# Adding the gathered row pieces of the last stage on GpSimd and VectorE instead of on TensorE and VectorE

## The chip, the cores and the metric

The kernel runs on one core of one Trainium2 chip. The metric is device time in microseconds for one launch, the median of several runs. The engines of the core are written as in the profile: PE (TensorE), DVE (VectorE), ACT (ScalarE), POOL (GpSimd), SP (SyncE, which here only issues DMAs). SBUF is the on-chip memory that all of them read, PSUM the memory that PE writes its sums to.

## The reference

A two-layer transformer for 512 tokens of width 1024 (and 256 context tokens in the first layer), each layer ending in a mixture of 64 experts of which every token uses 8. All of it is float32. What is touched here is the very end of the second layer: the weighted outputs of a token's 8 experts are summed, scaled by a gate, added to the residual stream, and the result is normalised.

```python
def body(acc, blk):                      # over blocks of rows of one expert
    tok, w, e = blk
    xb = x_pad[tok]
    h = jax.nn.silu(xb @ w_gate[e]) * (xb @ w_up[e])
    return acc.at[tok].add((h @ w_down[e]) * w[:, None]), None
...
y = moe_ffn(f_lat, *moe_args)            # routed + shared
h_lat = h_lat + gt_fl * y.reshape(b, n, d)
...
return rmsnorm(h_lat, g_final)
```

## The kernel before

The program is a row of stages. Six of them (named A to I in the tiles' names) are attention and projections; a stage E ends each layer with the experts. It is `stage_moe(l, nt, ...)`, called with `nt = 6` tiles of 128 tokens in layer 0 and `nt = NL = 4` in layer 1. The second call is the last stage of the program, and there `final` is true. Only code under `final` is concerned.

The experts' stage works on groups `g = 0 ... NGR-1` of 128 rows (a row is one token for one expert). POOL gathers a group's rows by an indirect DMA, PE transposes them and multiplies them by the gate and up weights (L1618) and the down weights (L1632), ACT scales the result by the routing weight (L1786), and POOL scatters the 128 rows to `y_d` in DRAM by an indirect DMA (L1493), each to place token*8 + k. In the last stage the last three groups (`KEPT = 3`) are not scattered: their results stay in SBUF, as `kept[j]` (the tiles `E_yb` and `E_tmp`).

Then comes the tail, which sums for each tile `t = 0 ... 3` of 128 tokens the 8 rows of each token:

- SP loads 16 pieces of 1 MB, four a tile, each 128 tokens x 2 of the 8 rows x 1024 (L1464). Piece `n` of tile `t` lies in `y[t][n]` and bumps its own semaphore `s_p[4t+n]`. The pieces go where expert weights lay before (`E_gu`, `E_dn`, `fT`, `h`, `o`), so SP waits for the down product of that expert before it issues a piece. SP works in the order of the program and is the only issuer of these loads.
- DVE adds the pieces `n < PIECES - on_pe[t]` into `y[t][0]` (L1992, 128x2048 each), and then its two halves onto each other (L1993, 128x1024). With `on_pe = [1, 1, 2, 2]` it adds three pieces in tiles 0 and 1, that is two instructions, and two pieces in tiles 2 and 3, that is one.
- PE adds the last `on_pe[t]` pieces into PSUM by multiplying with the identity (L1742, 4 matmuls a piece in the code) and, in `add_kept`, the rows of the three kept groups by multiplying with a 0/1 matrix that picks a token's row (L1750, 6 matmuls a tile). The sum lies in `psA[t % 2]` (`E_psX` for tiles 0 and 2, `E_psG` for 1 and 3). From tile 2 on PE first waits for `s_acc >= 2(t-1)`, which DVE raises when it has read the buffer of two tiles ago.
- DVE normalises the tile before (`normed(t-1)`: reciprocal L1983 and a scaled product L1986, from `h` and `gain` in `E_tmp`), then, for each half `b` of 512 columns: add PE's sum from PSUM (L2002), multiply by the gate in `E_xT` (L2003), add into the residual `h` (L2004). ACT squares and sums `h` (L1850) and takes the root (L1851), which the next `normed` waits for. SP stores the tile (L1467).

`link` is a `Chain`: each linked DVE instruction raises a semaphore and DVE waits for it before it issues the next one. POOL has nothing to do in the tail: its last instruction is the last scatter, after which it waits for the scatters to land.

Of the kernel before, what the change touches and what calls it, by code (L numbers as in the profile page):

```python
# [11 lines left out]
ALU = mybir.AluOpType  # L12
# [7 lines left out]
NL, NT = SEQ // P, (SEQ + CTX) // P  # L20
# [12 lines left out]
NE, NG, TOPG, TOPK, FF = 64, 8, 4, 8, 256  # L33
# [123 lines left out]
def build(nc, a, out):  # L157
    with ExitStack() as whole:
# [8 lines left out]
        def sem(name):  # L167
            held.append(nc.alloc_semaphore(name))
            return held[-1]
# [16 lines left out]
        ident = cst[:, C_ID:C_ID + P]  # L186
# [33 lines left out]
        def bc(ap, n):  # L220

            return ap.unsqueeze(1).to_broadcast([ap.shape[0], n, ap.shape[1]])

        def bcl(ap, n):

            return ap.unsqueeze(len(ap.shape)).to_broadcast(list(ap.shape) + [n])
# [1038 lines left out]
        def stage_moe(l, nt, fT, lg, sel, su, o, raw):  # L1265
# [9 lines left out]
            NGR, runs = plan.groups, plan.runs  # L1275
# [3 lines left out]
            final = nt == NL  # L1279
            KEPT = 3 if final else 0  # L1280
            with ExitStack() as ctx:
                S = lambda n: sem(f"E{l}_{n}_s")
# [38 lines left out]
                v = flat[:, 0:nt * NE].rearrange("p (t e) -> p t e", e=NE)  # L1321
# [35 lines left out]
                if final:  # L1357
                    hot = T("hot", [P, NL, P])
                    hots = [[hot[:, t] for t in range(NL)], [x[:].rearrange("p t e -> p (t e)")[:, i * P:(i + 1) * P] for x in (lg, sel) for i in range(2)],
                            [x.rearrange("p t e -> p (t e)")[:, i * P:(i + 1) * P] for x, n in ((wt[:], 2), (tab[:], 1), (xi[:].bitcast(F32), 1)) for i in range(n)]]  # L1360
                    hotc = T("hotc", [P, KEPT, NL])
                    st = T("st", [P, NL, 3])
                    gate, gain = xT[:].rearrange("p k n -> p (k n)"), xb[:, (NGR - 3) % XB]
                    kept = [yb[:, (NGR - 3) % 2], yb[:, (NGR - 2) % 2], xb[:, (NGR - 2) % XB]]
                    psA = [psX[:].rearrange("p b k n -> p b (k n)"), psG[:]]
                    PIECES, on_pe = TOPK // 2, [1, 1, 2, 2]
                    homes = []
                    for p in range(NE - ring, NE):
                        gu, dn = slots[p % ring]
                        if p % ring == SHARED:  # L1370
                            gu, dn = None, None
                            whole = o[:].rearrange("p t d -> p (t d)")
                            homes += [(p, whole[:, 2 * D * n:2 * D * n + 2 * D]) for n in range(3)]
                        else:
                            two = gu.rearrange("p m k n -> p (m k n)")
                            homes += [(p, two[:, 0:2 * D]), (p, two[:, 2 * D:4 * D]), (p, dn.rearrange("p k n -> p (k n)"))]
                    homes = [(p, x.rearrange("p (k d) -> p k d", k=2)) for p, x in homes]
                    an = homes[PIECES * NL][1]
                    y = [[homes[PIECES * t + n][1] for n in range(PIECES)] for t in range(NL)]
                    choice_rows = y_d[1].rearrange("(t p k) d -> t p k d", p=P, k=TOPK)  # L1380
                    s_p = [S(f"p{n}") for n in range(PIECES * NL)]
                    s_hot, s_v, s_pe = S("hot"), S("v"), S("pe")
                    s_h, s_rt, s_an, s_acc, s_out, s_act = S("h"), S("rt"), S("an"), S("acc"), [S("out0"), S("out1")], S("act")

                s_wd_, s_gt, s_fold = S("wd_"), S("gt"), S("fold")
# [8 lines left out]
                s_xa, s_xv, s_sil, s_mul, s_hT, s_y = (S(n) for n in ("xa", "xv", "sil", "mul", "hT", "y"))  # L1394
# [10 lines left out]
                with nc.Block(no_gpsimd_drain=True) as block:  # L1405
# [72 lines left out]
                    def _(pool):  # L1478
                        G = nc.gpsimd
# [59 lines left out]
                                rows_out(g % 2, sca[:, g - 2:g - 1], s_sc[g % 2])  # L1539
                        for j in range(2):  # L1540
                            pool.wait_ge(s_sc[j], 16 * ((NGR - KEPT - j + 1) // 2))

                    @block.tensor
                    def _(pe):
# [189 lines left out]
                        for t in range(NL):  # L1734
                            if t >= 2:
                                pe.wait_ge(s_acc, 2 * (t - 1))
                            def add_pieces():
                                for n in range(PIECES - on_pe[t], PIECES):
                                    pe.wait_ge(s_p[PIECES * t + n], 16)
                                    for b in range(2):  # L1740
                                        for k in range(2):
                                            ins = nc.tensor.matmul(psA[t % 2][:, b], ident, y[t][n][:, k, b * 512:(b + 1) * 512],  # L1742
                                                                   start=(t == 0 and n == PIECES - on_pe[t] and k == 0), stop=(t > 0 and n == PIECES - 1 and k == 1))
                                return ins

                            def add_kept():
                                for b in range(2):
                                    for j in range(KEPT):
                                        pe.wait_ge(s_y, NGR - KEPT + j + 1)
                                        ins = nc.tensor.matmul(psA[t % 2][:, b], hots[j][t], kept[j][:, b * 512:(b + 1) * 512],  # L1750
                                                               start=(t > 0 and j == 0), stop=(t == 0 and j == KEPT - 1))
                                return ins

                            if t == 0:
                                add_pieces()
                                add_kept().then_inc(s_pe, 1)
                            else:
                                add_kept()
                                add_pieces().then_inc(s_pe, 1)

                    @block.scalar
                    def _(act):
# [91 lines left out]
                    def _(dve):  # L1854
                        link = Chain(dve, s_dve)
                        V = nc.vector
# [50 lines left out]
                        for t in range(nt):  # L1907
                            ins = V.max(v8[:, t], v[:, t])
                        link(ins)
                        for t in range(nt):  # L1910
                            ins = V.tensor_tensor(eq[:, t], v[:, t].unsqueeze(1).to_broadcast([P, 8, NE]), bcl(v8[:, t], NE), ALU.is_equal)
                        link(ins)
                        for t in range(nt):
                            ins = V.tensor_tensor(eq[:, t], eq[:, t], bc(wt[:, t], 8), ALU.mult)
# [47 lines left out]
                        for g in range(NGR):  # L1962
# [5 lines left out]
                            if final and g == 2:  # L1968
                                for j in range(KEPT):
                                    n = NGR - KEPT + j  # L1970
                                    for t in range(NL):
                                        ins = V.tensor_scalar(hotc[:, j, t:t + 1], gat[:, n:n + 1], -float(t * P), None, ALU.add)
                                link(ins)
                                for j in range(KEPT):
                                    for t in range(NL):
                                        ins = V.tensor_scalar(hots[j][t], cst[:, C_COL:C_COL + P], hotc[:, j, t:t + 1], None, ALU.is_equal)
# [4 lines left out]
                        def normed(t):  # L1981
                            dve.wait_ge(s_rt, t + 1)
                            link(V.reciprocal(st[:, t, 2:3], st[:, t, 1:2]))  # L1983
                            if t >= 2:
                                dve.wait_ge(s_out[t % 2], 16 * (t // 2))
                            V.scalar_tensor_tensor(an[:, t % 2], h[:, t], st[:, t, 2:3], gain, ALU.mult, ALU.mult).then_inc(s_an, 1)  # L1986

                        for t in range(NL):
                            for n in range(PIECES - on_pe[t]):
                                dve.wait_ge(s_p[PIECES * t + n], 16)  # L1990
                                if n >= 1:
                                    link(V.tensor_tensor(y[t][0], y[t][0], y[t][n], ALU.add))  # L1992
                            link(V.tensor_tensor(y[t][0][:, 0], y[t][0][:, 0], y[t][0][:, 1], ALU.add))  # L1993
                            if t == 0:
                                dve.wait_ge(s_v, 32)
                            if t >= 1:
                                normed(t - 1)
                            for b in range(2):
                                c = slice(b * 512, (b + 1) * 512)
                                ac = y[t][0][:, 0, c]  # L2000
                                dve.wait_ge(s_pe, t + 1)
                                link(V.tensor_tensor(ac, ac, psA[t % 2][:, b], ALU.add))  # L2002
                                link(V.tensor_tensor(ac, ac, gate[:, c], ALU.mult))  # L2003
                                V.tensor_tensor(h[:, t, c], h[:, t, c], ac, ALU.add).then_inc(s_acc, 1)  # L2004
                            dve.wait_ge(s_acc, 2 * t + 2)
                            dve.sem_inc(s_h, 1)
# [593 lines left out]
```

## Time and profile before

| | |
|---|---|
| median of 3 runs | 2600.85 us (2596.98, 2600.85, 2615.37) |
| profiled execution: its time, its span | 2595.15 us, 2593.4 us |
| PE busy | 2347.7 us, 91% |
| DVE busy | 836.2 us, 32% |
| ACT busy | 664.7 us, 26% |
| POOL busy | 272.9 us, 11% |
| HBM traffic over the span | 261 GB/s |
| mean granted PE clock | 0.968 |

The shares are averages over the whole program. The tail that is changed lies between about 2530 us and the end, some 60 of 2593 us, so the argument is made in that stretch alone. The profile ends 1.75 us before the profiled execution's own time, and that execution lies 5.7 us under the median.

### The profile page before, as it was taken

How to read it: one execution, taken by the hardware profiler on the slowest of the kernel's cores; microseconds unless marked ns; L12 is line 12 of the kernel's file. 1: busy time of each engine (PE TensorE's matmuls, PEld its weight loads, DVE VectorE, ACT ScalarE, POOL GpSimd, SP SyncE). 2: the span in 40 equal slices, each digit the busy share in tenths (PEclk: the TensorE clock that was granted, in tenths of full speed). 3: DMA queues.
4: the chain of work that ended last, by engine and by line, in shares of the span. 5: the costliest groups of instructions: out<-in, count | busy, mean ns of one | idle time of the engine just before them, and what ended most of it. 6: DMA issues, size and time to landing. Idle time of an engine off the chain costs nothing. (4 is left out here: it accounts for less than half of the span.)

```text
span 2593.4 us, 34211 instructions
## 1 busy us (share of the span) xinstructions
PE 2347.7 (91%) x13502; PEld 1242.5 (48%) x13502; DVE 836.2 (32%) x1740; ACT 664.7 (26%) x1443; POOL 272.9 (11%) x257
## 2 busy tenths in 40 slices
PE   7999999799899999999994779998889998889888
PEld 3544555475544333333331778887645333333333
DVE  2332556626510001000013955556363100000006
ACT  1111444521011211212112344445311121111111
POOL 1000000032011111111111000000111111111100
PEclk9999999999999999999997899999989999999999
DMA  8565900112479999999995711100337999999996
GB/s 334 196 228 202 345 23 1 70 65 111 186 288 357 378 382 397 390 371 384 381 336 210 274 45 38 37 31 1 143 126 312 413 419 419 419 419 410 413 373 281
DMA packets 130093, 661.90 MB, mean 255 GB/s; under 512 B 18691, under 2 KB 29955, under 8 KB 68240
## 3 DMA queue, kind: packets, MB, share of 16 engines
q1 hardware_dynamic: 101120, 574.04, 56.7%
q0 software_dynamic: 28816, 85.69, 8.4%
q8 instruction: 108, 1.77, 0.3%
q14 instruction: 49, 0.40, 0.0%
HBM read 604.38 MB, written 72.96 MB: 261 GB/s over the span
## 5 line engine op out<-in xcount | busy, mean ns | idle before, releaser
L1618 PE MATMUL E_psG<-E_gu,E_xT 128*32 128x512 f32 (+2 forms) x2544 | 530.4, 611 | 45.3 <-DMA E_gu<-in_we_up_dram 29.8
L1952 DVE TENSOR_TENSOR E_hh<-E_sil,E_psG 128x256 f32<-128x256 f32 x96 | 40.5, 422 | 1078.5 <-ACT E_sil L1780 1078.5
L1618 PEld LDWEIGHTS E_psG<-E_gu,E_xT 128*32 128x32 f32 (+2 forms) x2544 | 158.1, 122 | 286.5 <-issue 279.7
L1632 PE MATMUL E_psY<-E_dn,E_hT 128*32 128x512 f32 (+2 forms) x1272 | 261.9, 596 | 1.5 <-ACT E_hT L1783 1.5
L1618 PE MATMUL E_psG<-fT,E_xT 128*32 128x512 f32 (+2 forms) x704 | 237.4, 619 | 3.7 <-DMA E_gu<-in_we_up_dram 3.2
L1618 PE MATMUL E_psG<-o,E_xT 128*32 128x512 f32 (+2 forms) x736 | 225.8, 612 | 5.7 <-DMA E_gu<-in_we_up_dram 5.7
L1780 ACT ACTIVATE E_sil<-E_psG 128x256 f32<-128x256 f32 x96 | 36.8, 383 | 657.7 <-PE E_psG L1618 657.7
L1493 POOL DMA_INDIRECT y_d<-E_yb,E_sca x91 | 91.5, 1006 | 951.2 <-ACT E_yb L1786 951.2
L1786 ACT ACTIVATE E_yb<-E_psY,E_wgt 128x1024 f32<-128x1024 f32 x95 | 105.8, 1114 | 285.7 <-PE E_psY L1632 285.7
L1618 PE MATMUL E_psG<-raw,E_xT 128*32 128x512 f32 (+2 forms) x464 | 148.4, 594 | 1.2 <-DVE E_xT L1949 1.2
L150 PE MATMUL I_psC<-I_w_hi,I_aT_hi 128*128 128x384 f32 (+1 forms) x336 | 111.4, 332 | 20.0 <-DVE I_aT_lo L2293 16.5
L1611 PEld LDWEIGHTS E_psX<-cst,E_tmp 128*128 128x128 f32 x768 | 94.2, 193 | 73.2 <-issue 72.8
L660 PE MATMUL B_psC<-w_in,B_aT 128*128 128x288 f32 (+3 forms) x384 | 122.0, 473 | 2.0 <-ACT B_aT L404 2.0
L1632 PEld LDWEIGHTS E_psY<-E_dn,E_hT 128*32 128x32 f32 (+2 forms) x1272 | 71.9, 118 | 105.3 <-issue 97.8
L1632 PE MATMUL E_psY<-o,E_hT 128*32 128x512 f32 (+2 forms) x368 | 112.6, 596 | 0.0
L1611 PE MATMUL E_psX<-cst,E_tmp 128*128 128x128 f32 x768 | 109.2, 285 | 0.0
L151 PE MATMUL I_psC<-I_w_lo,I_aT_hi 128*128 128x384 f32 (+1 forms) x336 | 107.6, 320 | 0.0
L152 PE MATMUL I_psC<-I_w_hi,I_aT_lo 128*128 128x384 f32 (+1 forms) x336 | 107.6, 320 | 0.0
L1488 POOL DMA_INDIRECT E_tmp<-f_d,E_gat x94 | 94.9, 1010 | 37.9 <-issue 36.9
L932 ACT ACTIVATE C_prob<-C_psS,C_nmax 128x768 f32<-128x768 f32 (+3 forms) x96 | 67.7, 705 | 118.5 <-DVE C_nmax L874 60.6
L1192 POOL TENSOR_TENSOR h<-h,D_y 128x1024 f32<-128x1024 f32 x8 | 18.9, 2357 | 732.1 <-DVE D_y L1169 732.1
L1618 PEld LDWEIGHTS E_psG<-fT,E_xT 128*32 128x32 f32 (+2 forms) x704 | 65.3, 126 | 62.3 <-issue 60.4
(452 smaller groups left out, 3789.0 us busy)
## 6 DMA issues: line engine op xcount, KB each, us to landing
E_gu<-in_we_gate_dram SPq DMA_DIRECT2D x70, 1024.0 KB, 14.3
E_gu<-in_we_up_dram SPq DMA_DIRECT2D x70, 1024.0 KB, 21.3
E_dn<-in_we_down_dram SPq DMA_DIRECT2D x70, 1024.0 KB, 16.0
h<-in_w_ada_dram SPq DMA_DIRECT2D x40, 1024.0 KB, 4.8
o<-in_we_gate_dram SPq DMA_DIRECT2D x24, 1024.0 KB, 11.9
o<-in_we_up_dram SPq DMA_DIRECT2D x24, 1024.0 KB, 15.7
o<-in_we_down_dram SPq DMA_DIRECT2D x24, 1024.0 KB, 24.0
I_ring<-y_d SPq DMA_DIRECT2D x24, 1024.0 KB, 7.1
```

The costliest lines, as they stand in the source:

```text
L150: nc.tensor.matmul(acc, xh, wh, start=(start and i == 0), stop=False)
L151: nc.tensor.matmul(acc, xh, wl, start=False, stop=False)
L152: ins = nc.tensor.matmul(acc, xl, wh, start=False, stop=(stop and i == n - 1))
L660: ins = nc.tensor.matmul(acc[:, 0:n], aT[:, k], w_in[:, k, c0:c0 + n], start=(k == 0), stop=(k == KD - 1))
L932: nc.scalar.activation(prob[:, i % 3, 0:len(ks) * P], psS[:, i % 2, c0:512 + CTX], ACT.Exp, bias=nmax[:, Q, u:u + 1], accum_out=ssum[:, Q, ...
L1488: pool.indirect_dma_start(xb[:, j], None, f_d[l][0:nt * P], bass.IndirectOffsetOnAxis(ap=index.bitcast(U32), axis=0), bounds_check=nt * P ...
L1493: pool.indirect_dma_start(y_d[l], bass.IndirectOffsetOnAxis(ap=index.bitcast(U32), axis=0), yb[:, j], None, bounds_check=nt * P * TOPK - 1 ...
L1611: ins = nc.tensor.transpose(psX[:, k // 4, k % 4], x[:, k], ident)
L1618: ins = nc.tensor.matmul(psG[c:c + n, 0].rearrange("p (v f) -> p v f", v=2), xT[:, k, c:c + n], slots[s][0][:, :, k], start=(k == 0), stop ...
L1632: ins = nc.tensor.matmul(psY[c:c + w, n], hT[:, j, k, c:c + w], slots[s][1][:, k, n * 512:(n + 1) * 512], start=(k == 0), stop=(k == KF - 1))
L1786: nc.scalar.activation(rows.rearrange("p (b n) -> p b n", b=2), psY[:], ACT.Copy, scale=wgt[:, i]).then_inc(done, 1)
L1952: V.tensor_tensor(hh[:], sil[:], psG[:, 0, FF:2 * FF], ALU.mult).then_inc(done, 1)
```

## The change

`on_pe` is gone. In each of the four tiles

- POOL adds piece 1 into piece 0 (`y[t][0] += y[t][1]`), after waiting for the two pieces' landings, and raises the new semaphore `s_pair`,
- DVE waits for pieces 2 and 3, adds 3 into 2, waits for `s_pair`, adds piece 2 into piece 0, and adds the halves as before,
- PE adds the kept rows alone.

```diff
-                    PIECES, on_pe = TOPK // 2, [1, 1, 2, 2]
+                    PIECES = TOPK // 2
...
                         for j in range(2):
                             pool.wait_ge(s_sc[j], 16 * ((NGR - KEPT - j + 1) // 2))
+                        if final:
+                            for t in range(NL):
+                                for n in range(2):
+                                    pool.wait_ge(s_p[PIECES * t + n], 16)
+                                G.tensor_tensor(y[t][0], y[t][0], y[t][1], ALU.add).then_inc(s_pair, 1)
...
-                            def add_pieces():
-                                for n in range(PIECES - on_pe[t], PIECES):
-                                    pe.wait_ge(s_p[PIECES * t + n], 16)
-                                    for b in range(2):
-                                        for k in range(2):
-                                            ins = nc.tensor.matmul(psA[t % 2][:, b], ident, y[t][n][:, k, b * 512:(b + 1) * 512],
...
-                            if t == 0:
-                                add_pieces()
-                                add_kept().then_inc(s_pe, 1)
-                            else:
-                                add_kept()
-                                add_pieces().then_inc(s_pe, 1)
+                            for b in range(2):
+                                for j in range(KEPT):
+                                    pe.wait_ge(s_y, NGR - KEPT + j + 1)
+                                    ins = nc.tensor.matmul(psA[t % 2][:, b], hots[j][t], kept[j][:, b * 512:(b + 1) * 512], start=(j == 0), stop=(j == KEPT - 1))
+                            ins.then_inc(s_pe, 1)
...
                         for t in range(NL):
-                            for n in range(PIECES - on_pe[t]):
+                            for n in range(2, PIECES):
                                 dve.wait_ge(s_p[PIECES * t + n], 16)
-                                if n >= 1:
-                                    link(V.tensor_tensor(y[t][0], y[t][0], y[t][n], ALU.add))
+                            link(V.tensor_tensor(y[t][2], y[t][2], y[t][3], ALU.add))
+                            dve.wait_ge(s_pair, t + 1)
+                            link(V.tensor_tensor(y[t][0], y[t][0], y[t][2], ALU.add))
                             link(V.tensor_tensor(y[t][0][:, 0], y[t][0][:, 0], y[t][0][:, 1], ALU.add))
```

Place 1 is DVE at tile 2. Before (`E_dn`, `E_gu`, `E_gu`, `E_dn` are the tile's four pieces in order):

```order
L1992 TENSOR_TENSOR E_dn<-E_dn,E_gu 128x2048
L1993 TENSOR_TENSOR E_dn<-E_dn 128x1024
L1983 RECIPROCAL E_st<-E_st 128x1
L1986 SCALAR_TENSOR_TENSOR o<-h,E_st,E_tmp 128x1024
L2002 TENSOR_TENSOR E_dn<-E_dn,E_psX 128x512
```

and with the change:

```order
L1978 TENSOR_TENSOR E_gu<-E_gu,E_dn 128x2048
L1980 TENSOR_TENSOR E_dn<-E_dn,E_gu 128x2048
L1981 TENSOR_TENSOR E_dn<-E_dn 128x1024
L1970 RECIPROCAL E_st<-E_st 128x1
L1973 SCALAR_TENSOR_TENSOR o<-h,E_st,E_tmp 128x1024
```

DVE has one 128x2048 addition more here, and so in tile 3; in tiles 0 and 1 the count is the same, two, but the first of them now adds pieces 2 and 3.

Place 2 is PE at tiles 2 (`E_psX`) and 3 (`E_psG`), behind the kept rows. Before:

```order
L1750 MATMUL E_psX<-E_tmp,E_tab 128x512
L1742 MATMUL E_psX<-E_gu,cst 128x512 x4
L1742 MATMUL E_psX<-E_dn,cst 128x512 x4
L1750 MATMUL E_psG<-E_yb,E_hot 128x512
```

and with the change, the whole of tile 3 and the end of tile 2:

```order
L1745 MATMUL E_psX<-E_tmp,E_tab 128x512
L1745 MATMUL E_psG<-E_yb,E_hot 128x512
L1745 MATMUL E_psG<-E_yb,sel 128x512
L1745 MATMUL E_psG<-E_tmp,E_xi 128x512
L1745 MATMUL E_psG<-E_yb,E_hot 128x512
L1745 MATMUL E_psG<-E_yb,sel 128x512
L1745 MATMUL E_psG<-E_tmp,E_xi 128x512
```

The 24 matmuls by the identity (`cst`), 4 for each of 6 pieces, are gone. Place 3 is POOL behind its last two scatters, where nothing stood before:

```order
L1493 DMA y_d<-E_yb,E_sca 4096x1024 x2
L1546 TENSOR_TENSOR E_gu<-E_gu 128x2048
L1546 TENSOR_TENSOR fT<-fT,h 128x2048
L1546 TENSOR_TENSOR E_dn<-E_dn,E_gu 128x2048
L1546 TENSOR_TENSOR E_gu<-E_gu 128x2048
```

Four additions are new there, one a tile, both inputs in SBUF. The order of SP's DMAs is the same in both kernels.

## Rows read from the trace of the kernel before

**Rows 1.** The chain of waits, 2530 to 2594 us: start us, us, what

```profile
2540.50 3.63 PE E_psX L1742 x8
...
2575.03 6.88 PE E_psG L1742 x16
...
2587.92 1.28 DVE o L1986
```

**Rows 2.** The timeline of DVE, 2532 to 2594 us: start us, us, instruction

```profile
2537.47 2.29 DVE L1992 TENSOR_TENSOR E_gu<-E_gu,E_dn 128x2048 f32<-128x2048 f32 x1 [0.42 <-DMA E_dn<-y_d]
...
2549.42 0.69 DVE L2002 TENSOR_TENSOR E_gu<-E_gu,E_psX 128x512 f32<-128x512 f32 x1 [8.40 <-PE E_psX L1750]
...
2553.83 2.29 DVE L1992 TENSOR_TENSOR fT<-fT,h 128x2048 f32<-128x2048 f32 x1 [0.23 <-DVE h L2004]
...
2558.49 1.23 DVE L1993 TENSOR_TENSOR fT<-fT 128x1024 f32<-128x1024 f32 x1
...
2561.15 0.68 DVE L2002 TENSOR_TENSOR fT<-fT,E_psG 128x512 f32<-128x512 f32 x1
...
2565.55 2.29 DVE L1992 TENSOR_TENSOR E_dn<-E_dn,E_gu 128x2048 f32<-128x2048 f32 x1 [0.22 <-DVE h L2004]
...
2581.93 0.69 DVE L2002 TENSOR_TENSOR E_gu<-E_gu,E_psG 128x512 f32<-128x512 f32 x1 [1.93 <-PE E_psG L1742]
...
2585.43 0.69 DVE L2004 TENSOR_TENSOR h<-h,E_gu 128x512 f32<-128x512 f32 x1
```

**Rows 3.** The timeline of SP's DMA issues, 2500 to 2594 us

```profile
2533.28 0.43 SPq L1464 DMA_DIRECT2D h<-y_d  x1
2535.40 0.92 SPq L1464 DMA_DIRECT2D E_gu<-y_d  x2
...
2536.95 0.96 SPq L1464 DMA_DIRECT2D E_gu<-y_d  x2
...
2540.54 1.83 SPq L1464 DMA_DIRECT2D E_gu<-y_d  x2
...
2544.57 1.34 SPq L1464 DMA_DIRECT2D o<-y_d  x1
```

**Rows 4.** DMA issues in windows inside rows 3: KB each, us to landing

```profile
h<-y_d SPq DMA_DIRECT2D x1, 1024.0 KB, 14.3
...
E_gu<-y_d SPq DMA_DIRECT2D x1, 1024.0 KB, 16.8
...
E_gu<-y_d SPq DMA_DIRECT2D x1, 1024.0 KB, 20.6
...
E_gu<-y_d SPq DMA_DIRECT2D x1, 1024.0 KB, 26.6
...
o<-y_d SPq DMA_DIRECT2D x1, 1024.0 KB, 27.9
```

**Rows 5.** POOL's groups by form: xcount | busy us, mean ns | idle before

```profile
L1192 POOL TENSOR_TENSOR h<-h,D_y 128x1024 f32<-128x1024 f32 x8 | 18.9, 2357 | 732.1 <-DVE D_y L1169 732.1
L1505 POOL TENSOR_TENSOR o<-o,E_yb 128x2048 f32<-128x2048 f32 x2 | 9.0, 4498 | 6.7 <-DMA E_yb<-mod_d 6.6
```

**Rows 6.** The timelines of DVE and of POOL where both worked, layer 1

```profile
1883.07 2.49 DVE L1126 TENSOR_TENSOR o<-lg,D_brt 128x128 f32<-128x128 f32 x1
1887.05 0.29 DVE L1136 TENSOR_TENSOR o<-o 128x128 f32<-128x128 f32 x1
1922.98 0.23 DVE L1888 TENSOR_TENSOR E_bst<-E_psX,E_tab 128x64 f32<-128x64 f32 x1
...
1883.01 2.40 POOL L1194 TENSOR_TENSOR D_f<-D_f,D_fadd 128x1024 f32<-128x1024 f32 x1 [3.11 <-DVE D_f L1181]
...
1922.67 4.49 POOL L1505 TENSOR_TENSOR o<-o,E_yb 128x2048 f32<-128x2048 f32 x1 [6.58 <-DMA E_yb<-mod_d]
```

**Rows 7.** The same two timelines, layer 0

```profile
527.24 1.22 DVE L1107 TENSOR_TENSOR D_oTl<-o,D_oTh 128x1024 fp32r<-128x1024 f32 x1
...
527.41 3.31 POOL L1194 TENSOR_TENSOR D_f<-D_f,D_fadd 128x1024 f32<-128x1024 f32 x1 [4.40 <-DVE D_f L1181]
```

More of the change, by code:

```diff
@@ L1381, in stage_moe @@
                     s_p = [S(f"p{n}") for n in range(PIECES * NL)]
-                    s_hot, s_v, s_pe = S("hot"), S("v"), S("pe")
+                    s_pair, s_hot, s_v, s_pe = S("pair"), S("hot"), S("v"), S("pe")
                     s_h, s_rt, s_an, s_acc, s_out, s_act = S("h"), S("rt"), S("an"), S("acc"), [S("out0"), S("out1")], S("act")
@@ L1736, in _ @@
                                 pe.wait_ge(s_acc, 2 * (t - 1))
-                            def add_pieces():
-                                for n in range(PIECES - on_pe[t], PIECES):
-                                    pe.wait_ge(s_p[PIECES * t + n], 16)
-                                    for b in range(2):
-                                        for k in range(2):
-                                            ins = nc.tensor.matmul(psA[t % 2][:, b], ident, y[t][n][:, k, b * 512:(b + 1) * 512],
[L1743 to L1752, printed above, removed]
-                            if t == 0:
-                                add_pieces()
-                                add_kept().then_inc(s_pe, 1)
-                            else:
-                                add_kept()
-                                add_pieces().then_inc(s_pe, 1)
+                            for b in range(2):
[3 more added lines that the diff above has]
+                            ins.then_inc(s_pe, 1)
                     @block.scalar
```

## The prediction

> **What bounds the kernel now.** The page's shares say PE, but they are means over 2593 us. The change lies behind the last group of experts, so I read the chain of waits from 2530 us on first. It is PE without a gap, from the first matmul by the identity at 2540.50 to the last pair of pieces at 2575.03 + 6.88 = 2581.9 [rows 1]. Behind it follow DVE's six gate instructions of tile 3, a root on ACT and the last product at 2587.92. So the tail is bound by PE today, and the change takes PE work off that chain. The question is what is late next.
>
> DVE's timeline answers it. DVE stands idle before PE's sum twice: 8.40 us in tile 0 and 1.93 us in tile 3 [rows 2]. In tiles 1 and 2 it has no idle time beyond 0.23 us. So DVE is nearly as late as PE, and only those two waits can be won.
>
> The third view is the landings. A piece lands at its issue in [rows 3] plus the time in [rows 4]: tile 1's piece 1 (`h`) at 2533.28 + 14.3 = 2547.6, its piece 3 (second of the pair at 2535.40, so issued at about 2535.9) at + 16.8 = 2552.7, tile 2's piece 1 at 2536.95 + 20.6 = 2557.6, tile 3's piece 1 (second of the pair at 2540.54, about 2541.0) at + 26.6, about 2567.5, and the last piece at 2544.57 + 27.9 = 2572.5. SP's order is the same in both kernels and its waits are on PE's groups, which the change leaves alone, so these times stay.
>
> **What is removed from PE.** One piece costs 3.44 us (16 records for two pieces take 6.88 [rows 1]). Six pieces go: 20.6 us of PE. The kept rows stay. They end for tile 0 at about 2546.0 instead of 2549.4 (3.63 us earlier, the time from 2540.50 that tile 0's piece held PE). Later tiles' kept rows wait only for `s_acc` of two tiles ago and take some 5 us, 10 at half the clock, against 7 us or more of DVE work before they are read: hidden.
>
> **What DVE does after, POOL's additions left out.** From the start of a tile's first 2048-wide addition to the next tile's start, with two such additions, `normed` and the six gate instructions: 2565.55 - 2553.83 = 11.72 us, of which 2561.15 - 2553.83 = 7.32 us lie before the PSUM addition [rows 2]. Tile 0 starts when its piece 3 is there, about 2540.1, and gets to the PSUM addition at 2546.0. It would be through at 2550.4 (4.4 us of gate). Tile 1 has to wait: today its first addition wants pieces 0 and 1, with the change pieces 2 and 3, and piece 3 lands at 2552.7. So most of the gain in tile 0 is lost to the landing. From 2552.8 on DVE runs three full tiles, since tiles 2 and 3 now have two wide additions as well: tile 2 at 2564.5, tile 3 at 2576.2, its last gate instruction starting at 2576.2 + 10.8 = 2587.0. Today that is 2585.43 [rows 2]. So even with POOL's work free, the end moves by **+1.6 us**: two additions of 2.33 us more, 3.0 us of waits and starts less. Below zero is excluded: landings and DVE's durations are both given by rows.
>
> **What POOL's additions cost.** They are 128x2048 additions with both inputs in SBUF. POOL's rows are 4.498 us for a 2048-wide and 2.357 us for a 1024-wide instruction [rows 5]; I take 4.5. Pair 0 runs at 2534.8 to 2539.3, before DVE's first addition: hidden. For the others the question is whether DVE can work beside them, and the trace has an answer in stages that this change does not touch. At 1883.07 DVE began a 128x128 addition from SBUF while POOL's L1194 had just begun. It took 2.49 us where its like takes 0.29, and ended 0.15 us after POOL's instruction [rows 6]. The other way round, POOL's L1194 began at 527.41 beside a DVE subtraction of two SBUF tensors, which ended at 528.46; it took 3.31 us, which is 2.26 us counted from DVE's end [rows 7]. A DVE addition with one input in PSUM (L1888, 0.23 us at 1922.98) ran freely beside POOL's L1505 [rows 6]. So of the instructions in the tail, everything but L2002 and the tiny reciprocal excludes POOL's additions, and the engine that comes second waits for the whole of the other's instruction.
>
> I place the three additions by that:
> - Pair 1 is wanted at 2547.6, during DVE's L2003/L2004 of tile 0. POOL gets in at about 2548.1 and holds until 2552.6. DVE's second PSUM addition runs beside it; L2003 and L2004 follow, and tile 1 starts at 2554.3 instead of 2552.8: +1.5 us.
> - Pair 2 is wanted at 2557.6, inside tile 1's second wide addition (2556.6 to 2558.9). POOL then holds 2558.9 to 2563.4, and the halves' addition waits: +4.5 us.
> - Pair 3 is wanted at about 2567.5, between gate instructions of tile 1. It is exposed less one PSUM addition: +3.9 us.
>
> Together +9.9 us, and with the +1.6 of above **+11.4 us** after rounding. Bounds: no exclusion gives +1.6; three additions wholly on the path give 1.6 + 13.5 = +15.1. I stay at 11.4, since the trace shows both directions of the exclusion for just this kind of instruction. The new wait for `s_pair` costs nothing by itself: each pair is done before DVE's second wide addition asks for it. Behind it on DVE is all the rest of the tile. POOL's wait for the pieces has nothing queued behind it.
>
> The profiled execution would be 2595.15 + 11.4 = 2606.6 us. The median of the runs lies 5.7 us above that execution, so the forecast is 2600.85 + 11.4, about **2612 us**.
>
> **The notes.** The exclusion and its extent are read from the rows above alone. The Trainium skill's page "Advanced Engine Details and Errata", section "VectorE Performance Modes", names only the two-port modes of VectorE as blocking GpSimd; a plain float32 addition of two tensors is in none, and by that rule the sum would be +1.6. The page "SBUF — State Buffer", section "Who interferes with whom", also counts VectorE instructions with two SBUF inputs against a GpSimd instruction that reads SBUF, and by it the sum would be about +11. The trace sides with the second: 2.49 against 0.29 us.
>
> **The rivals.**
> - *POOL and DVE work side by side.* The wide additions are plain float32 ones, and the two DVE rows above could have had other reasons. Then +1.6 us: 2602.5, which no measurement here tells from no change. Against it: rows 6 and 7 agree to 0.15 us with an instruction-long exclusion. Chance 0.10.
> - *POOL comes in late.* DVE's linked instructions leave about 0.03 us between them. If POOL does not get in there, it runs only when DVE itself stops at `s_pair`, in every tile from 1 on and with its start-up: three additions wholly exposed and some 1 us of hand-over each, 1.6 + 13.5 + 3 = +18, about 2619. Chance 0.08.
> - *Slower by over 1%.* If POOL's stretched row (3.31 us for 1024 elements) is its own rate when DVE is busy, a pair takes 6.6 us. Four of them on the path give 1.6 + 26.5 = +28, about 2629. It decides from a POOL addition of 6.1 us on with all four exposed ((26 - 1.6) / 4). Against it: the unhurried rows of 2.35 and 4.5 us, and pair 0 has no DVE work beside it. Chance 0.03.
> - *Faster.* PE's 20.6 us off the chain become a gain if DVE's tile 1 need not wait for its pieces and POOL is free. The rows leave 1.9 and 3.4 us of waits to win at the most, against 4.7 us of added DVE work. Chance 0.02, all of it within 1%.
>
> **How the numbers follow.** The forecast has 0.77. The range takes in the free case (2602.5) and the late POOL (2619); to both ends I add some 3 us, since the median of three runs moves by about that (two of the three runs lie 4 us apart): **2599 to 2622**. What is left out is the slow case, part of the late one, and a median drawn up by a run like the 2615. About 1% (26 us) is what a measurement of this kernel can tell from no change, and nearly every case lies inside it: faster by over 1% 0.01, within 1% 0.94, slower by over 1% 0.05.
>
> **What would show it.** Right: PE no longer in the chain behind 2550 us; DVE first waiting for piece 3 of tile 1 or for POOL; three DVE instructions with two SBUF inputs, one each near 2549, 2559 and 2568 us, that last 3.5 to 6 us instead of 0.7 or 1.2; POOL's rows at 4.5 to 5 us for the first and up to 6.8 when it came second; the last `normed` starting some 11 us later. Wrong: DVE durations unchanged (the first rival), POOL rows over 6 us with no DVE row beside them (the third), long idle time on DVE put down to POOL (the second), or pieces that land earlier or later than before by over 2 us, which would move all of it.

## The result and the profile after

Over 20 runs each, the changed kernel takes 2615.67 us in the median (2605.69 to 2624.78) and the kernel before 2602.92 us (2594.74 to 2615.37). The ratio is 1.0044 with a 95% interval of 1.003 to 1.0059, that is +11.5 us (7.8 to 15.4). It comes from the undisturbed runs and is not the quotient of the two medians, which lie 12.75 us apart. The forecast was +11.4 us and 2612 us. The profiled execution has a span of 2603.9 us, 10.5 us over the span of before.

A run varies by some 10 us either way, and most of that lies ahead of the tail: in the profiles of the eight experiments below, PE's first matmul of the tail lies anywhere from 2541.8 to 2558.5 us. So I measure the tail. Each kernel has one profile, so how much a tail varies by itself is not measured; the part that can be read is DVE's wait for tile 1's piece 3, which was anything from none to 2.7 us. Differences between tails of 1 or 2 us are therefore not told from scatter, while the lengths of single rows repeat to 0.1 us. The tail runs from the start of PE's first matmul behind the last group to the end of DVE's last addition into `h`. Before it is 2540.43 to 2586.12, **45.7 us**. With the change it is 2540.97 to 2596.62, **55.7 us**: +10.0 us. The rest of the 10.5 us is the 0.5 us by which the tail starts later.

DVE's timeline of the changed kernel, 2530 to 2604 us (start us, us, instruction), answers to [rows 2]:

```profile
2546.52 0.69 DVE L1990 TENSOR_TENSOR E_gu<-E_gu,E_psX 128x512 f32<-128x512 f32 x1 [3.12 <-PE E_psX L1745]
2547.25 3.32 DVE L1991 TENSOR_TENSOR E_gu<-E_gu,E_xT 128x512 f32<-128x512 f32 x1
...
2553.57 2.29 DVE L1978 TENSOR_TENSOR E_gu<-E_gu 128x2048 f32<-128x2048 f32 x1 [0.22 <-DVE h L1992]
2555.89 6.48 DVE L1980 TENSOR_TENSOR fT<-fT,E_gu 128x2048 f32<-128x2048 f32 x1
2562.40 1.23 DVE L1981 TENSOR_TENSOR fT<-fT 128x1024 f32<-128x1024 f32 x1
...
2565.78 4.65 DVE L1991 TENSOR_TENSOR fT<-fT,E_xT 128x512 f32<-128x512 f32 x1
2570.46 0.69 DVE L1992 TENSOR_TENSOR h<-h,fT 128x512 f32<-128x512 f32 x1
...
2573.43 2.29 DVE L1978 TENSOR_TENSOR E_gu<-E_gu,E_dn 128x2048 f32<-128x2048 f32 x1 [0.22 <-DVE h L1992]
2575.75 2.29 DVE L1980 TENSOR_TENSOR E_dn<-E_dn,E_gu 128x2048 f32<-128x2048 f32 x1
...
2595.93 0.69 DVE L1992 TENSOR_TENSOR h<-h,E_gu 128x512 f32<-128x512 f32 x1
```

POOL's timeline in the same stretch, where the kernel before has nothing:

```profile
2532.61 4.52 POOL L1546 TENSOR_TENSOR E_gu<-E_gu 128x2048 f32<-128x2048 f32 x1 [26.40 <-DMA E_gu<-y_d]
2545.50 4.51 POOL L1546 TENSOR_TENSOR fT<-fT,h 128x2048 f32<-128x2048 f32 x1 [8.38 <-DMA h<-y_d]
2555.45 4.77 POOL L1546 TENSOR_TENSOR E_dn<-E_dn,E_gu 128x2048 f32<-128x2048 f32 x1 [5.43 <-DMA E_gu<-y_d]
2565.39 4.50 POOL L1546 TENSOR_TENSOR E_gu<-E_gu 128x2048 f32<-128x2048 f32 x1 [5.17 <-DMA E_gu<-y_d]
```

Read the two side by side. Three DVE rows are long: 3.32 instead of 0.69 us, 6.48 instead of 2.29, 4.65 instead of 0.69. Together that is 2.63 + 4.19 + 3.96 = 10.8 us. Each spans the end of a POOL row and ends about its own normal length later: the 3.32 us row ends at 2550.57, POOL's at 2550.01. (Taken back by its normal length, each held row would have started 0.13 to 0.15 us before POOL's row ends.) No idle time stands ahead of these rows. A hold of this kind is part of the instruction's duration, and a list of waits doesn't show it. POOL was second once: it was ready at 2555.45, the DVE addition before it ended at 2555.86, and POOL's row is 4.77 us. DVE's next addition, issued at 2555.89, then had to wait for POOL. The first of the four POOL additions (tile 0's) ended at 2537.13, before DVE began, and held nobody. Where POOL has nothing to do, DVE's rows have their old length (2.29 us at 2573.43 and 2575.75).

The chain of waits from 2530 us on (start us, us, what) answers to [rows 1]:

```profile
2541.04 5.36 PE E_psX L1745 x12
...
2555.89 6.49 DVE fT L1980
...
2565.78 4.66 DVE fT L1991
...
2598.43 1.28 DVE o L1973
```

PE is out of it after tile 0's kept rows. From 2546.5 us on the chain is DVE to its last addition into `h`; behind that come ACT's squares and root and DVE's last product, as in the kernel before.

### The profile page after: what moved, and what is told of

Read it like the earlier page. It is cut to its first block and busy times, and to the rows that moved or that the text cites. A ratio compares the mean times of both kernels' runs of the same rounds, so it can differ in the third digit from the quotient of the medians.

```text
span 2603.9 us, 34126 instructions
## 1 busy us (share of the span) xinstructions
PE 2328.6 (89%) x13454; PEld 1232.0 (47%) x13454; DVE 850.1 (33%) x1742; ACT 665.9 (26%) x1443; POOL 292.2 (11%) x261
## 3 DMA queue, kind: packets, MB, share of 16 engines
q1 hardware_dynamic: 101120, 574.04, 56.6%
```

## The experiments

All tails are measured as above, each in one profile. For the change the ratio is over 20 runs of each kernel, for the experiments that have one it is over 10 or 12 runs against 17 to 19 of the kernel before. Pair on DVE, pair left out, POOL only writes and POOL in halves ran on one chip; POOL twice, gate in PSUM and the change in tile 0 on a second; POOL copies, built when the memsets had been seen, on a third.

| kernel | tail, us | holds on DVE rows, us | ratio to before, 95% |
|---|---|---|---|
| before | 45.7 | none | 1 |
| the change | 55.7 | 2.63 + 4.19 + 3.96 | 1.0044 [1.003, 1.0059] |
| pair on DVE | 52.9 | none | 1.0029 [1.0006, 1.0052] |
| pair left out | 45.8 | none | 1.0017 [0.9993, 1.0041] |
| POOL only writes | 47.5 | none | one run |
| POOL copies | 49.0 | 0.91 + 1.60 + 1.57 | one run |
| POOL in halves | 56.6 | six of 1.6 to 2.1 | one run |
| POOL twice | 70.5 | seven of 3.5 to 4.2 | one run |
| gate in PSUM | 55.7 | 2.87 + 4.18 + 3.26 | one run |
| change in tile 0 alone | 42.6 | none | 0.9996 [0.9978, 1.0013] |

**The pair on DVE.**

```diff
-                                G.tensor_tensor(y[t][0], y[t][0], y[t][1], ALU.add).then_inc(s_pair, 1)
...
-                            for n in range(2, PIECES):
+                            for n in range(PIECES):
                                 dve.wait_ge(s_p[PIECES * t + n], 16)
                             link(V.tensor_tensor(y[t][2], y[t][2], y[t][3], ALU.add))
-                            dve.wait_ge(s_pair, t + 1)
+                            link(V.tensor_tensor(y[t][0], y[t][0], y[t][1], ALU.add))
```

> The changed kernel with DVE adding the first pair too; POOL idle in the tail. 'Tail' is from PE's first matmul behind the last group to the end of DVE's last addition into h: 45.6 us before, 55.6 us with the change. Theory (DVE and POOL exclude each other): the three held-up DVE instructions (2.63 + 4.19 + 3.96 = 10.8 us of extra length) become normal and three additions of 2.33 us come onto DVE's path; the fourth, in tile 0, is hidden under PE's kept rows. Tail 55.6 - 10.8 + 7.0 = 51.8 us. Rival (POOL did not hold DVE up; the tail is long for another reason, such as landings or PE): DVE has 7 us more to do, tail 62.6 us.

Measured: tail 2558.48 to 2611.33 = 52.9 us, 1.1 us over the figure of the theory and 9.7 under that of the rival. Part of the 1.1 us is a wait for tile 1's piece 3 (0.69 us idle, where 0.2 is usual). Giving DVE 7 us more work made the tail 2.8 us shorter, since POOL's three additions had cost DVE 10.8. In the medians this kernel (2611.2 us) and the change (2615.67) cannot be told apart: the intervals of their ratios overlap.

**The pair left out.**

```diff
-                                G.tensor_tensor(y[t][0], y[t][0], y[t][1], ALU.add).then_inc(s_pair, 1)
...
-                            for n in range(2, PIECES):
+                            for n in range(PIECES):
                                 dve.wait_ge(s_p[PIECES * t + n], 16)
                             link(V.tensor_tensor(y[t][2], y[t][2], y[t][3], ALU.add))
-                            dve.wait_ge(s_pair, t + 1)
```

> The changed kernel with nobody adding piece 1 of a tile (a quarter of the routed rows that were not kept is left out of the sums); POOL idle in the tail. This is the free-POOL case of the prediction, which put it at 1.6 us over the kernel before. Theory: all DVE rows at their normal length, tail 55.6 - 10.8 = 44.8 us, or up to 47.2 us if tile 1's piece 3 lands as late as in the kernel before. Rival (the length has another cause): tail stays near 55.

Measured: 2551.43 to 2597.24 = 45.8 us, inside the range of the theory. So of the 10.0 us that the change adds, 9.9 go away with POOL's additions. What remains, the removal of PE's matmuls for two DVE additions more, moved the tail by 0.1 us here. The prediction had +1.6 us; the difference is the landing of tile 1's piece 3, which made DVE wait 0.95 us here instead of some 2.4.

**POOL only writes.**

```diff
-                                G.tensor_tensor(y[t][0], y[t][0], y[t][1], ALU.add).then_inc(s_pair, 1)
+                                G.memset(y[t][1], 0.0)
+                                G.memset(y[t][0], 0.0).then_inc(s_pair, 1)
```

> The changed kernel with each of POOL's additions replaced by two memsets of 128x2048 to the same two pieces (pieces 0 and 1 are so left out of the sums), some 3.7 us together from the 0.96 us of a 128x1024 memset in the trace of before. Theory in its narrow form (only a POOL instruction that reads SBUF excludes a DVE instruction with two SBUF inputs): no DVE row is longer than normal, tail about 45 us. Rival (any POOL access to SBUF excludes): DVE rows held up by up to 1.9 us each behind a memset, tail 50 to 54 us.

Two pairs of rows from the timelines of POOL and of DVE in this kernel show it:

```profile
2549.36 1.80 POOL L1546 MEMSET h<- 128x2048 f32 x1 [9.64 <-DMA h<-y_d]
2551.11 1.80 POOL L1547 MEMSET fT<- 128x2048 f32 x1
2559.30 1.80 POOL L1546 MEMSET E_gu<- 128x2048 f32 x1 [6.39 <-DMA E_gu<-y_d]
...
2550.95 0.69 DVE L1993 TENSOR_TENSOR h<-h,E_gu 128x512 f32<-128x512 f32 x1
2554.34 2.29 DVE L1979 TENSOR_TENSOR E_gu<-E_gu 128x2048 f32<-128x2048 f32 x1 [2.69 <-DMA E_gu<-y_d]
...
2558.99 1.22 DVE L1982 TENSOR_TENSOR fT<-fT 128x1024 f32<-128x1024 f32 x1
2560.24 0.17 DVE L1971 RECIPROCAL E_st<-E_st 128x1 f32<-128x1 f32 x1
2560.44 1.29 DVE L1974 SCALAR_TENSOR_TENSOR o<-h,E_st,E_tmp 128x1024 f32<-128x1024 f32 x1
```

The DVE rows at 2550.95, 2558.99 and 2560.44 run under a memset of POOL, all with two SBUF inputs, all at their normal length, and the memsets keep their 1.80 us as well. Tail 47.5 us (2541.80 to 2589.25), with the 2.69 us wait for tile 1's piece 3 in it. So it is not POOL's being busy or its writing that excludes. This is also the free-POOL case as the prediction worked it out, landing and all: +1.8 us, forecast +1.6.

**POOL copies.**

```diff
-                                G.tensor_tensor(y[t][0], y[t][0], y[t][1], ALU.add).then_inc(s_pair, 1)
+                                G.tensor_copy(y[t][0], y[t][1]).then_inc(s_pair, 1)
```

> The changed kernel with each of POOL's additions replaced by a copy of piece 1 onto piece 0 (one SBUF input, one output; piece 0 is so left out of the sums). The run with memsets showed no hold at all (tail 47.4 us, 2.7 us of it a wait for tile 1's piece 3), so writing alone is free. If reading by POOL is what excludes DVE, rows with two SBUF inputs are held up here too, each by at most the copy's own length (estimated at 2 to 3 us from 0.85 us for 768 elements in the trace of before), and the tail is 47 to 52 us. Rival (only POOL instructions with two inputs exclude): no DVE row longer than normal.

The first two held-up DVE rows and POOL's copies, from their timelines:

```profile
2555.17 1.60 DVE L1991 TENSOR_TENSOR E_gu<-E_gu,E_xT 128x512 f32<-128x512 f32 x1
...
2564.42 2.82 DVE L1981 TENSOR_TENSOR fT<-fT 128x1024 f32<-128x1024 f32 x1
...
2554.34 1.89 POOL L1546 COPY fT<-h 128x2048 f32<-128x2048 f32 x1 [10.86 <-DMA h<-y_d]
2564.27 1.89 POOL L1546 COPY E_dn<-E_gu 128x2048 f32<-128x2048 f32 x1 [8.04 <-DMA E_gu<-y_d]
2574.21 2.90 POOL L1546 COPY E_gu<-E_gu 128x2048 f32<-128x2048 f32 x1 [8.05 <-DMA E_gu<-y_d]
```

Holds again, of up to 1.6 us, and POOL's last copy was itself held 1.0 us by the DVE addition that ended at 2575.37. Tail 2548.90 to 2597.85 = 49.0 us. One input that POOL reads is enough, and the hold is what is left of POOL's instruction, less some 0.15 us (0.91 of 1.06, 1.60 of 1.74, 1.57 of 1.71 us).

**POOL in halves.**

```diff
-                                G.tensor_tensor(y[t][0], y[t][0], y[t][1], ALU.add).then_inc(s_pair, 1)
+                                G.tensor_tensor(y[t][0][:, 0], y[t][0][:, 0], y[t][1][:, 0], ALU.add)
+                                G.tensor_tensor(y[t][0][:, 1], y[t][0][:, 1], y[t][1][:, 1], ALU.add).then_inc(s_pair, 1)
```

> The changed kernel with POOL's addition of a tile in two of 128x1024 (2.35 us each). Theory (whole-instruction exclusion, and the engine that waits gets in at the next gap): the holds become shorter, at most 2.4 us a row, and more in number, two for each of the pairs 1 to 3, the engines taking turns; the tail stays within 1.5 us of 55.6 us. Rival (DVE wins back time with smaller POOL instructions, since part of a pair falls into times when DVE reads PSUM or waits): tail under 53 us. Rival (bandwidth is shared, not locked): no single long DVE rows, all rows inside POOL's spans longer by the same share.

DVE's timeline around tile 1's pair, and POOL's:

```profile
2563.24 4.32 DVE L1981 TENSOR_TENSOR fT<-fT,E_gu 128x2048 f32<-128x2048 f32 x1
2567.59 3.25 DVE L1982 TENSOR_TENSOR fT<-fT 128x1024 f32<-128x1024 f32 x1
...
2562.94 2.47 POOL L1546 TENSOR_TENSOR E_dn<-E_dn,E_gu 128x1024 f32<-128x1024 f32 x1 [4.84 <-DMA E_gu<-y_d]
2565.37 4.39 POOL L1547 TENSOR_TENSOR E_dn<-E_dn,E_gu 128x1024 f32<-128x1024 f32 x1
```

The engines take turns, one instruction each: POOL's second half is issued at 2565.37, waits for DVE's wide addition to end at 2567.56, and then holds DVE's next one. Six holds of 1.6 to 2.1 us add up to 11.8 us; tail 2547.37 to 2603.98 = 56.6 us, as expected. Halving POOL's instructions gives nothing back. It also rules out shared bandwidth: that would have stretched all rows under POOL's alike, and not one row of 0.69 us to 2.7 beside a row with a PSUM input that keeps its length.

**POOL twice.**

```diff
+                                G.tensor_tensor(y[t][1], y[t][0], y[t][1], ALU.add).then_inc(s_pair, 1)
+                                pool.wait_ge(s_pair, 2 * t + 1)
                                 G.tensor_tensor(y[t][0], y[t][0], y[t][1], ALU.add).then_inc(s_pair, 1)
...
-                            dve.wait_ge(s_pair, t + 1)
+                            dve.wait_ge(s_pair, 2 * t + 2)
```

> The changed kernel with POOL doing a second 128x2048 addition in each tile ahead of its own (piece 1 += piece 0, then piece 0 += piece 1, so the sums are off): twice the suspected cost. Theory: tile 0's is hidden under PE; the three others add up to 4.5 us each to the 10.8 us of holds, less what falls into PSUM reads: tail 55.6 + 9 to 13.5, that is 65 to 69 us. Rival (POOL's work is beside DVE's): tail near 55.6 us as long as a pair of 9 us is ready when DVE asks for it.

Measured: 2543.48 to 2613.97 = 70.5 us, 14.8 us over the change, and a little over the expected range. The reason is tile 0: there the second POOL addition reached into DVE's time (its first wide addition is 6.04 us instead of 2.29), which I had put down as hidden. Without those 3.75 us the tail would be 66.7 us, inside the range. Seven DVE rows are held, by 3.5 to 4.2 us each. Twice the POOL work more than doubles the loss: 24.7 us over the tail with no pair, where the change has 9.9.

**The gate in PSUM.**

```diff
+                        nc.scalar.activation(gateP[0], gate[:, 0:512], ACT.Copy)
+                        nc.scalar.activation(gateP[1], gate[:, 512:1024], ACT.Copy).then_inc(s_gp, 1)
...
-                                link(V.tensor_tensor(ac, ac, gate[:, c], ALU.mult))
+                                link(V.tensor_tensor(ac, ac, gateP[b], ALU.mult))
```

> The changed kernel with the gate copied to two free PSUM banks by ACT, so that the product with the gate reads one SBUF and one PSUM input. It asks whether it is the number of SBUF inputs of the DVE instruction that decides. Theory: none of the eight gate products is longer than 0.7 us; the two holds that fell on them move to the addition into h that follows, shorter by the 0.7 us of the product; the hold on the second wide addition stays; tail about 54.2 us. Rival (any DVE instruction is held up beside POOL): the products are held up as before, tail 55.6 us.

`gateP` stands for the two free banks, `psS` and `psH`; its definition and the waits of ACT and DVE are not shown.

DVE's timeline at the end of tile 0, and POOL's row that belongs to it:

```profile
2553.96 0.68 DVE L1996 TENSOR_TENSOR E_gu<-E_gu,E_psX 128x512 f32<-128x512 f32 x1
2554.67 0.69 DVE L1997 TENSOR_TENSOR E_gu<-E_gu,E_psH 128x512 f32<-128x512 f32 x1
2555.39 3.56 DVE L1998 TENSOR_TENSOR h<-h,E_gu 128x512 f32<-128x512 f32 x1
...
2553.54 4.86 POOL L1546 TENSOR_TENSOR fT<-fT,h 128x2048 f32<-128x2048 f32 x1 [8.42 <-DMA h<-y_d]
```

The gate product, now with one SBUF and one PSUM input, runs in 0.69 us inside POOL's row; the addition into `h` behind it, with two SBUF inputs, waits until POOL is through. All eight products are 0.69 us. So for the same product of two tensors, one input moved from SBUF to PSUM is enough to let it through, as expected. The tail did not become shorter, though: 2546.18 to 2601.87 = 55.7 us instead of 54.2. The three holds (10.3 us) are only 0.5 us less than in the change, and DVE's wait for tile 1's piece 3 (0.59 us, where 0.22 is usual) and a start of the gate that is 0.2 us later make up for that. POOL's requests fell at other instants. In the change the first came at 2545.50, while DVE waited for PE, so that 1.0 us of POOL's addition passed before DVE had work; here it came during an addition into `h`, so that POOL's addition began at about 2553.9; 1.4 us of it passed under the PSUM addition and the product, and 2.87 fell on DVE. The second fell on the addition of the halves and not, as expected, on the second wide one. The freed product is worth up to 0.7 us a hold, and where the request falls moves a hold by as much or more.

**The change in tile 0 alone.**

```diff
-                    PIECES, on_pe = TOPK // 2, [1, 1, 2, 2]
+                    PIECES, on_pe = TOPK // 2, [0, 1, 1, 2]
...
+                            for n in range(2):
+                                pool.wait_ge(s_p[n], 16)
+                            G.tensor_tensor(y[0][0], y[0][0], y[0][1], ALU.add).then_inc(s_pair, 1)
...
```

> The kernel before with the change made in tile 0 alone, where POOL's addition falls into a time in which DVE has nothing to add, and with PE adding 0, 1, 1 and 2 pieces in the four tiles instead of 1, 1, 2 and 2. Theory: POOL's addition is over before DVE starts; PE reaches tile 0's sum 3.4 us earlier and has two pieces (6.9 us) less in all; DVE has one wide addition more, in tile 2. Worked out from the landings of the kernel before: DVE's last tile reaches PE's sum at 2578.8 instead of 2581.9, so the tail is 42.5 us, 3.1 us under the kernel before, a ratio of 0.9988 that runs can hardly resolve. Rival (POOL's addition costs wherever it stands, or tile 1's landings eat the lead of tile 0): tail 45 us or more.

In tile 0 DVE and PE work as in the change; those lines are not shown.

POOL's only row of the tail, and from DVE's timeline its first row and its last addition into `h`:

```profile
2542.41 4.51 POOL L1545 TENSOR_TENSOR E_gu<-E_gu 128x2048 f32<-128x2048 f32 x1 [26.96 <-DMA E_gu<-y_d]
...
2547.53 2.29 DVE L1995 TENSOR_TENSOR E_dn<-E_dn,fT 128x2048 f32<-128x2048 f32 x1 [5.44 <-DMA fT<-y_d]
...
2591.57 0.69 DVE L2013 TENSOR_TENSOR h<-h,E_gu 128x512 f32<-128x512 f32 x1
```

POOL is done at 2546.92, 0.6 us before DVE starts. Tail 2549.71 to 2592.26 = 42.6 us, 3.1 us under the kernel before and as worked out. The medians are 2600.19 us against 2599.52, a ratio of 0.9996 with an interval of 0.9978 to 1.0013: 3 us of 2600 cannot be seen in the whole time. By the trace it is the shortest of the tails; as a faster kernel it is not shown. How much of the 3.1 us needs POOL is not separated either: no run gives tile 0's pair to DVE with PE's pieces placed like this.

## Why the prediction was right

- *The bound.* PE's chain was the bound before and DVE became it. The chain after is DVE from 2546.5 us on, as forecast. One wait was not in the forecast: it had DVE start tile 0 at 2540.1 and reach PE's sum just as it was ready. Tile 0's piece 3 came earlier, DVE started at 2537.53 and stood idle for PE's sum for 3.12 us, which cost nothing.
- *The cost without POOL (+1.6 us).* The two experiments that keep the change's DVE work and have no hold give +0.1 us (pair left out) and +1.8 us (POOL only writes). The forecast leaned on tile 1's piece 3 landing 12.3 us behind PE's first tail matmul, as in the trace before, and called a cost below zero excluded. That landing is not fixed. DVE waited 2.69 us for the piece in the kernel with memsets, 0.95 with the pair left out, 0.69 with the pair on DVE, and not at all in the changed kernel. There the DMA view gives the piece 14.0 us from its issue at about 2536.5, so it landed at 2550.5, 9.5 us behind the mark. Less its holds the changed kernel's tail is 55.7 - 10.8 = 44.9 us, 0.8 *under* the kernel before. So this term was mis-sized: -0.8 us in this execution instead of +1.6.
- *The exclusion.* The forecast took it from two places in stages that the change does not touch [rows 6, 7]. It held with its limits: an addition or product with a PSUM input goes through, a POOL instruction that reads SBUF holds to its end, and the second to come waits.
- *The three holds.* Forecast were additions to the path of 1.5, 4.5 and 3.9 us, 9.9 together. Measured are 2.63, 4.19 and 3.96, 10.8 together. The first was the one mis-sized: I let DVE's wait for tile 1's piece 3 absorb most of it. Without the hold DVE would have been through tile 0 at 2553.35 - 2.63 = 2550.7, when the piece had just landed, so there was nothing to absorb it.
- *The sum, and the luck in it.* In the tail -0.8 and 10.8 make +10.0 us instead of 11.4: one landing moved the first term down by 2.4 us and the first hold up by 1.1, so that its effect cancels in part. (The terms as written, 1.6 and 9.9, add up to 11.5, and 2549.4 less the 3.63 us named is 2545.8, not 2546.0; neither matters here.) That +11.4 stands beside +11.5 in the whole time is luck: the interval runs from 7.8 to 15.4, the medians lie 12.75 apart and the tail gives 10.0. The 2612 us rests on a median of three runs, 2600.85; over 20 runs the kernel before takes 2602.92.
- *What would show it.* Three long DVE rows with two SBUF inputs were forecast near 2549, 2559 and 2568 us; they stand at 2547.25, 2555.89 and 2565.78. They last 3.32, 6.48 and 4.65 us where 3.5 to 6 was written; the second is on the wide addition and not on the halves. POOL's rows were 4.5 to 4.8 us, under the 6.8 us that I had allowed for the one that comes second. One of the signs of being wrong came up as well, pieces that land over 2 us earlier: POOL begins pairs 1 to 3 at 2545.50, 2555.45 and 2565.39, where 2547.6, 2557.6 and 2567.5 were written, 2.1 us earlier each time. All three moved together, which is why the pattern stayed.
- *The rivals.* Side by side: refuted, the rows are held. POOL late, with DVE never letting it in: refuted, POOL starts at the next gap between two linked DVE instructions, even one of 0.03 us. POOL at 6.6 us by its own rate: refuted, 4.5 us. A gain: no. (Its chance stands once as 0.02, all within 1%, and once as 0.01 for over 1%; the two do not fit.)

The Trainium skill's page "SBUF — State Buffer", section "Who interferes with whom", counts a VectorE instruction with two SBUF inputs against a GpSimd instruction that reads SBUF, and not against one that only writes. Both halves are borne out: holds of up to 4.2 us with POOL additions and 1.6 us with copies, none with memsets.

## What to carry to other kernels

Work given to an idle GpSimd costs VectorE nothing where GpSimd does not read SBUF, or where VectorE has nothing to run that is held by it. Held are additions and products of two tensors in SBUF, and not these alone (see the last section); otherwise a 4.5 us addition takes up to 4.2 us from VectorE to spare it 2.3 us. Look for the cost in the durations of the other engine's rows, since no wait shows it. And when work is taken off the engine that bounds a stretch, first find the idle time of the next one: here it was 3.4 + 1.9 us, and two additions of 2.3 us used up all but 0.7 us of it. Last, a landing time read from one execution is no constant: here one piece came 2.7 us earlier in the next, against the same mark.

## What was not expected of the hardware

A VectorE instruction with *one* input in SBUF can be held too. The trace of the kernel before shows it beside POOL's addition of 1922.67 to 1927.16 us [rows 6], and behind it an instruction of the same size that came when POOL was done:

```profile
1923.24 3.97 DVE L1889 TENSOR_SCALAR E_xi<-E_bst 128x64 int32<-128x64 f32 x1
1927.24 0.20 DVE L1890 TENSOR_SCALAR E_xi<-E_xi 128x64 int32<-128x64 int32 x1
```

Neither reads more than one tensor; the rest are constants. L1889 ends 0.05 us after POOL's addition, and so does its other execution (2.72 us at 630.79, POOL's end 633.46), and both in the changed kernel. A sum over one SBUF tensor of 64x64 (TENSOR_REDUCE, L1881, 0.21 us at 626.69) ran under a POOL addition at its usual length. So the number of SBUF inputs sorts the additions and products of the tail; it is not the whole rule. No run here varies a one-input instruction, so why this one is held stays open.

When both engines have work, they take turns, one instruction each. The prediction did not say so, the expectation of the halves did: two DVE rows in succession were held at each of the three places, by 1.6 to 2.1 us. Cutting POOL's work finer did not shorten the tail (+0.9 us, one profile each). And a POOL copy of 128x2048 float32 takes 1.89 us where the addition takes 4.5, so that the hold by a copy is under half of that by an addition.
